# Gate product of the last mixer taken in three rounded passes, with the low weight parts subtracted on the Pool engine

## The chip, the cores and the metric

The kernel runs on one core of a Trainium2 chip. The metric is the device time of one execution in microseconds (us), as the median of several runs. The engines are named as in the profile: PE multiplies matrices, PEld loads its weights, DVE is the vector engine, ACT the scalar engine, POOL (GpSimd) the third elementwise engine, which here has issued DMAs only, and SP issues the weight transfers.

## The reference, cut to what matters

The model is two blocks on 256 tokens of width 1024. The change lies in the mixer of the second block. All its projections come from one input `h`:

```
h = rms_norm(x, attn_norm_g)
proj = h @ w_in
q, k, v, qi, ki, wi, glu_in, gates = jnp.split(proj, ...)
y_att = dsa_attention(q, k, v, qi, ki, wi, rel_bias) @ w_att_out     # top-64 keys per query, then softmax
y_conv = conformer_conv(glu_in, conv_w, conv_b, ...)                 # depthwise convolution with 31 taps
g = jax.nn.sigmoid(gates + b_gate).reshape(B, S, 2, D)
mixed = g[:, :, 0, :] * y_att + g[:, :, 1, :] * y_conv
x = x + mixed @ w_out
```

`gates` is a product of 256x1024 by 1024x2048. After the mixer comes a stage that gathers rows of expert tables (over a third of the time), then an embedding and the output.

## The kernel before, in words

Every engine runs a program of its own, written out by hand, and waits on semaphores. There is no scheduler: an instruction waits for all that stands ahead of it on its engine.

**Weights** are read through `ring`, four slots of 128x2048 f32, which SP fills in the order of `UNITS`. A unit is two slots, and the gates have four units. SP refills a slot when `raw_free` says that it was read.

**Two ways to multiply.** A product named in `SPLIT` is done in rounded type (fp32r): ACT copies a slot to `whi`, rounded (L499); DVE subtracts `wlo = ring - whi` (L1290), which also frees the ring slot; then PE adds three passes, high by high, low input by high weight, high input by low weight. The input's own parts, `hTh` and `hTl`, stand ready since the norm. `whi` and `wlo` have two buffers each, so slot q waits until the product of slot q-2 is over (`split_used`). In a product that is also in `WIDE`, one slot holds half of the inner dimension for 512 output columns, and each matmul has 512 columns (L809, function `wide`). The other way, which `gates` uses before the change, is a full f32 product straight from `ring` (L799), each matmul with 256 columns, after a one-row matmul that adds the bias (L1089).

**Around the gates.** PE's order is: last projection (`qkv`), gate block 0, transposes of q and k, gate block 1, first logits (L1110, L1113), gate block 2, transposes of the first probabilities, the second logits in two halves, gate block 3, transposes of the second probabilities, attention times v, then transposes of the convolution's result, and the two output projections (L1158). DVE meanwhile normalises q and k (L1663, L1664), picks the top 64 keys (L1677, L1678), runs 124 taps of the convolution (L1621, L1624) in stretches between the steps of the attention, adds the mask to the logits (L1705, L1713), finds the maximum, and normalises the probabilities (L1693). ACT takes the exponentials (L694) and the sigmoid of each gate block (L687). PE may start block n only after the sigmoid of block n-2. POOL has one load between (`conv_ln_b`), and the next (`ffn_norm_g`) is not needed before the gather stage.

## Time and profile before

| | us |
|---|---|
| median of 3 runs | 1884.62 |
| the runs | 1887.63, 1884.62, 1881.87 |
| profiled execution, its own time | 1888.51 |
| span of the profiled execution | 1886.5 |
| mean granted PE clock of its span | 0.938 |

Of the span PE is busy for 1569.8 us (83%), DVE for 1062.4 (56%), ACT for 526.2 (28%), POOL for 504.9 (27%). On the chain that ended last PE has 52%, POOL 15%, DVE 14% and DMA 10%. These are averages over stages with different limits; the change lies in the 100 us from 980 to 1080, and that stage is read by itself. A time in brackets at a timeline row's end is how long the engine sat idle before it, with what ended the idling. "x16" counts instructions in the trace: an f32 matmul stands in it as two instructions, a rounded one as one.

### The profile page before, as it was taken

Reading aid. Unit: us, or ns where it says so; the run is one execution under the profiler, and the core shown is the slowest. Engines: PE = TensorE matmul, PEld = TensorE weight load, DVE = VectorE, ACT = ScalarE, POOL = GpSimd, SP = SyncE. Lnnn points to the kernel's source line nnn. Section 1 sums busy time; section 2 is a strip of 40 time slices with the busy share of each in tenths; the row PEclk is TensorE's granted clock in tenths of the full one; section 3 lists DMA queues with packets and bytes.
Section 4 is the critical chain, followed back from the end, with each engine's and each line's share of the span. In section 5 each row is a group of like instructions: output and inputs, shape, how many; then the busy total and the mean of one; then the engine's idle time right before and its main releaser. Section 6 shows DMA issues by size and latency. Waiting matters only on the chain.

```text
span 1886.5 us, 19976 instructions
## 1 busy us (share of the span) xinstructions
PE 1569.8 (83%) x8015; PEld 1115.1 (59%) x8015; DVE 1062.4 (56%) x1762; ACT 526.2 (28%) x674; POOL 504.9 (27%) x555
## 2 busy tenths in 40 slices
PE   3998669999996869996999879838777776997787
PEld 2887569987985769985977548812222222442234
DVE  1642655644447446544388545596667566665553
ACT  2350145434442244434241212112121212212111
POOL 2000000000000000000000000557777776777771
PEclk8898789999998879997899999969999998999999
DMA  8548555556755445564343235999999999999994
GB/s 314 183 136 314 198 181 182 186 188 226 255 198 192 154 179 178 179 194 157 113 142 109 78 134 207 404 417 418 418 418 419 418 418 373 414 417 418 419 419 179
DMA packets 116259, 497.22 MB, mean 264 GB/s; under 512 B 12280, under 2 KB 12416, under 8 KB 98640
## 3 DMA queue, kind: packets, MB, share of 16 engines
q0 software_dynamic: 77424, 284.26, 37.5%
q1 hardware_dynamic: 38752, 211.83, 32.3%
q8 instruction: 55, 0.90, 0.2%
q14 instruction: 28, 0.23, 0.0%
HBM read 494.98 MB, written 1.06 MB: 263 GB/s over the span
## 4 chain that ended last, share of the span: by engine, by line
PE 52%; POOL 15%; DVE 14%; DMA 10%; issue 6%; ACT 2%; POOLq 0%; SPq 0%; DVEq 0%; ACTq 0%
PE G L799 21%; PE G L809 20%; POOL late L477 8%; DMA ybuf<-in_peer_u,mod 6%; POOL mod L477 3%; PE M L1202 2%; POOL arena L477 2%; DMA ring<-in_wpack 2%; POOL ybuf L477 2%; PE G L1158 2%; PE T L799 1%; DVE mod L1852 1%; DVE late L1852 1%; DVE wlo L1290 1%; PE G L837 1%
## 5 line engine op out<-in xcount | busy, mean ns | idle before, releaser
L1290 DVE TENSOR_TENSOR wlo<-ring,whi 128x2048 fp32r<-128x2048 f32 x120 | 274.9, 2292 | 313.5 <-ACT whi L499 313.2
L499 ACT ACTIVATE whi<-ring 128x2048 fp32r<-128x2048 f32 x120 | 229.3, 1911 | 365.2 <-PE G L809 185.4
L1202 PE MATMUL M<-late,cB 128*128 128x512 f32 x480 | 232.6, 613 | 46.7 <-DMA late<-in_peer_v,mod 46.7
L1852 DVE SCALAR_TENSOR_TENSOR late<-late,G 128x1024 f32<-128x1024 f32 x128 | 154.6, 1219 | 108.7 <-DMA late<-in_peer_u,mod 108.5
L1202 PEld LDWEIGHTS M<-late,cB 128*128 128x128 f32 x480 | 83.5, 189 | 193.4 <-DMA late<-in_peer_v,mod 125.1
L749 ACT ACTIVATE cB<-consts,mod 128x128 f32<-128x128 f32 x240 | 90.2, 398 | 357.7 <-PE M L1202 354.1
L1202 PE MATMUL M<-mod,cB 128*128 128x512 f32 x240 | 121.6, 635 | 74.3 <-ACT cB L749 48.5
L477 POOL DMA_INDIRECT late<-in_peer_u,mod x128 | 121.3, 948 | 51.1 <-issue 33.3
L477 POOL DMA_INDIRECT late<-in_peer_v,mod x128 | 122.0, 953 | 40.0 <-issue 36.1
L1202 PEld LDWEIGHTS M<-mod,cB 128*128 128x128 f32 x240 | 43.3, 197 | 149.9 <-issue 84.3
L799 PE MATMUL G<-hTh,whi 128*128 128x256 f32 x800 | 117.5, 291 | 10.8 <-DVE hTl L1311 7.3
L799 PE MATMUL G<-hTl,whi 128*128 128x256 f32 x800 | 115.8, 289 | 0.0
L799 PEld LDWEIGHTS G<-hTh,whi 128*128 128x128 f32 x800 | 107.5, 200 | 12.0 <-issue 11.9
L799 PE MATMUL G<-hTh,wlo 128*128 128x256 f32 x800 | 114.4, 287 | 0.0
L799 PEld LDWEIGHTS G<-hTl,whi 128*128 128x128 f32 x800 | 106.9, 198 | 0.0
L799 PEld LDWEIGHTS G<-hTh,wlo 128*128 128x128 f32 x800 | 105.4, 196 | 0.0
L1852 DVE SCALAR_TENSOR_TENSOR mod<-mod,G 128x1024 f32<-128x1024 f32 x64 | 76.4, 1218 | 33.5 <-DMA mod<-in_peer_u,mod 33.1
L809 PE MATMUL G<-whi,fl 128*128 128x512 f32 x320 | 88.4, 398 | 5.1 <-DVE fh L1589 5.1
L809 PE MATMUL G<-whi,fh 128*128 128x512 f32 x320 | 88.2, 398 | 0.0
L407 POOL DMA_DIRECT2D arena<-in_norm_g x4 | 2.1, 536 | 303.7 <-DVE arena L1515 156.1
L902 PE MATMUL T<-consts,ybuf 128*128 128x128 f32 x112 | 26.7, 417 | 61.3 <-ACT ybuf L537 41.8
L477 POOL DMA_INDIRECT mod<-in_peer_u,mod x64 | 60.1, 939 | 55.8 <-DVE mod L1835 27.1
(356 smaller groups left out, 2512.4 us busy)
## 6 DMA issues: line engine op xcount, KB each, us to landing
ring<-in_wpack SPq DMA_DIRECT2D x200, 1024.0 KB, 5.1
mod<-in_ada_b POOLq DMA_DIRECT2D x4, 512.0 KB, 9.3
arena<-in_norm_g POOLq DMA_DIRECT2D x4, 512.0 KB, 7.3
late<-in_peer_u,mod POOLq DMA_INDIRECT x128, 9.4
late<-in_peer_v,mod POOLq DMA_INDIRECT x128, 9.3
xs<-in_x SPq DMA_DIRECT2D x1, 1024.0 KB, 13.1
arena<-in_wsT POOLq DMA_DIRECT2D x1, 1024.0 KB, 5.0
mod<-in_ln_g POOLq DMA_DIRECT2D x1, 1024.0 KB, 9.5
```

Source lines behind the costliest of these rows:

```text
L407: pool.dma_start(dst, src).then_inc(sem(name), 16)
L477: nc.gpsimd.indirect_dma_start(out=rowbufs[j].rearrange("p a n -> p (a n)"), out_offset=None, in_=(A["peer_u"], A["peer_v"])[kind], in_off ...
L499: nc.scalar.activation(whi[:, q % 2, :], ring[:, raw % RING, :], ACT.Copy).then_inc(hi_done, 1)
L749: nc.scalar.activation(diags[:, k % DIAGS, :], ident, ACT.Copy, scale=actv[:, t, n:n + 1]).then_inc(sem("diag_made"), 1)
L799: ins = nc.tensor.matmul(dst, lhs(k), rhs(k), start=(first and k == 0), stop=(last and k == DC - 1))
L809: ins = nc.tensor.matmul(dst, lhs(t, k0 + k), w[:, :, k, :], start=(first and n + k == 0), stop=(last and n == 2 and k == 3))
L837: ins = nc.tensor.matmul(dst, cB[:, k, 0:32], w[:, :, k, :, r], start=(k == 0), stop=(k == DC - 1))
L902: return lambda dst: nc.tensor.transpose(dst[0:src.shape[1], :], src, ident)
L1158: ins = nc.tensor.matmul(G[:, b % 2, t, :], xT[:, k, t * P:(t + 1) * P], w[:, k, :], start=(k == 0), stop=(k == 3))
L1202: ins = nc.tensor.matmul(M[:, nb, :], diags[:, k % DIAGS, :], rowbufs[g % GBUF][:, nb, :], start=(n == 0), stop=(n == NSEL - 1))
L1290: V.tensor_tensor(wlo[:, q % 2, :], ring[:, raw % RING, :], whi[:, q % 2, :].bitcast(F32), ALU.subtract).then_inc(raw_free[raw % RING], 1)
L1852: V.scalar_tensor_tensor(out=row, in0=row, scalar=1.0, in1=G[:, t, :, :], op0=ALU.mult, op1=ALU.mult, accum_out=dots[:, t, n:n + 1]).then_ ...
```

## The change

`gates` joins `SPLIT` and `WIDE`, so that its eight slots are laid out and multiplied as the other rounded products are. PE adds the bias with one 512-column matmul for each of the two token tiles, then runs `wide` for each half. ACT rounds the slots, two ahead of each block. The subtraction is given to POOL, which does all eight one after the other, in its queue behind the load of `conv_ln_b`. DVE's counter of slots skips eight. In ACT's program the high parts and the sigmoids of the next blocks stand ahead of the exponentials.

```
-SPLIT = (..., "qi", "qkv", "glu",
-         "out")
-WIDE = ("a_v", "a_o", "a_out", "b_v", "qkv", "out")
+SPLIT = (..., "qi", "qkv", "glu",
+         "gates", "out")
+WIDE = ("a_v", "a_o", "a_out", "b_v", "qkv", "gates", "out")
@@ gpsimd
+            def low(name, j=0):
+
+                q, raw = SPLIT0[name] + j, 2 * UNIT0[name] + j
+                pool.wait_ge(hi_done, q + 1)
+                nc.gpsimd.tensor_tensor(wlo[:, q % 2, :], ring[:, raw % RING, :], whi[:, q % 2, :].bitcast(F32),
+                                        ALU.subtract).then_inc(raw_free[raw % RING], 1)
...
             load(clnb, A["conv_ln_b"].partition_broadcast(P), "l_cln")
+            for j in range(8):
+                low("gates", j)
             pool.wait_ge(m_free, SPARE0["att"])
@@ scalar
-            gate_sigmoid(0)
-            exponentials(0)
-            for nb in (1, 2):
+            split("gates", 0)
+            for nb in range(4):
+                if nb < 3:
+                    split("gates", nb + 1)
                 gate_sigmoid(nb)
-            exponentials(1)
-            gate_sigmoid(3)
+                if nb in (1, 2):
+                    exponentials(nb - 1)
@@ tensor, gate_product(nb)
+                for t in range(TT):
+                    nc.tensor.matmul(G[:, b % 2, t, :], ones[0:1, :], bgrow[0:1, 512 * nb:512 * nb + 512],
+                                     start=True, stop=False)
                 for half in range(2):
-                    h, c0 = 2 * (UNIT0["gates"] + nb) + half, 512 * nb + 256 * half
-                    w = raw(h)
-                    for t in range(TT):
-                        dst = G[:, b % 2, t, 256 * half:256 * (half + 1)]
-                        nc.tensor.matmul(dst, ones[0:1, :], bgrow[0:1, c0:c0 + 256], start=True, stop=False)
-                        ins = product(dst, lambda k: hT[:, k, t * P:(t + 1) * P], lambda k: w[:, k, :], False)
-                    ins.then_inc(raw_free[h % RING], 1)
+                    h = 2 * (UNIT0["gates"] + nb) + half
+                    pe.wait_ge(raw_free[h % RING], h // RING + 1)
+                    wide(b, SPLIT0["gates"] + 2 * nb + half, 4 * half, lambda t, k: hTh[:, k, t * P:(t + 1) * P],
+                         lambda t, k: hTl[:, k, t * P:(t + 1) * P], False, half == 1)
@@ vector, ahead of split("out", 0)
+            made[0] += 8
```

Gate block 0 on PE, between the last projection and the transposes of q (`T<-consts,arena`), in the kernel before:

```order
603 L1089 MATMUL G<-ybuf,ones 128x256
604 L799 MATMUL G<-ring,hT 128x256 x8
605 L1089 MATMUL G<-ybuf,ones 128x256
606 L799 MATMUL G<-ring,hT 128x256 x8
607 L1089 MATMUL G<-ybuf,ones 128x256
608 L799 MATMUL G<-ring,hT 128x256 x8
609 L1089 MATMUL G<-ybuf,ones 128x256
610 L799 MATMUL G<-ring,hT 128x256 x8
611 L902 MATMUL T<-consts,arena 128x128 x16
```

and in the changed kernel, where `wide` stands at L819 and the bias at L1095:

```order
603 L1095 MATMUL G<-ybuf,ones 128x512 x2
604 L819 MATMUL G<-whi,hTh 128x512 x4
605 L819 MATMUL G<-whi,hTl 128x512 x4
606 L819 MATMUL G<-wlo,hTh 128x512 x4
...
615 L819 MATMUL G<-wlo,hTh 128x512 x4
616 L912 MATMUL T<-consts,arena 128x128 x16
```

36 matrix instructions of 256 columns have become 50 of 512, 48 of them in rounded type. Each of the four blocks changes in this way.

ACT from the last copy of `qkv` (`arena<-G`) to the second set of exponentials, before; `mod<-G` is a sigmoid, `mod,small<-mod,small` an exponential:

```order
161 L681 ACTIVATE arena<-G 128x1024
162 L687 ACT_TABLE_LOAD
163 L687 ACTIVATE mod<-G 128x2x512
164 L694 ACT_TABLE_LOAD
165 L694 ACTIVATE mod,small<-mod,small 128x128 x8
166 L687 ACT_TABLE_LOAD
167 L687 ACTIVATE mod<-G 128x2x512 x2
168 L694 ACT_TABLE_LOAD
169 L694 ACTIVATE mod,small<-mod,small 128x256 x8
```

and after:

```order
161 L690 ACTIVATE arena<-G 128x1024
162 L508 ACTIVATE whi<-ring 128x2048 x4
163 L696 ACT_TABLE_LOAD
164 L696 ACTIVATE mod<-G 128x2x512
165 L508 ACTIVATE whi<-ring 128x2048 x2
166 L696 ACTIVATE mod<-G 128x2x512
167 L703 ACT_TABLE_LOAD
168 L703 ACTIVATE mod,small<-mod,small 128x128 x8
169 L508 ACTIVATE whi<-ring 128x2048 x2
170 L696 ACT_TABLE_LOAD
171 L696 ACTIVATE mod<-G 128x2x512
172 L703 ACT_TABLE_LOAD
173 L703 ACTIVATE mod,small<-mod,small 128x256 x8
```

The last two high parts stand behind the first exponentials.

POOL behind the load of the gate bias (`ybuf`), before:

```order
31 L407 DMA ybuf<-in_b_gate 1x16x128
32 L407 DMA arena<-in_conv_ln_b 128x512
33 L407 DMA mod<-in_ffn_norm_g 128x1024
34 L407 DMA arena<-in_skT 128x2048
```

and after:

```order
31 L407 DMA ybuf<-in_b_gate 1x16x128
32 L407 DMA arena<-in_conv_ln_b 128x512
33 L413 ISA
34 L413 TENSOR_TENSOR wlo<-ring,whi 128x2048 x8
35 L407 DMA mod<-in_ffn_norm_g 128x1024
36 L407 DMA arena<-in_skT 128x2048
```

Eight subtractions and one more instruction, which sets up the engine's code for them, stand between two loads.

## Rows read from the trace of the kernel before

**Rows 1.** Busy time by engine from 980 to 1080 us: busy, count, granted clock, DMA.

```profile
980.00:1080.00 100.00, 93.46 (x444) 68.92 (x444) 74.96 (x183) 20.25 (x44) 0.53 (x1) 1.00 0.26 90
```

**Rows 2.** PE's timeline: last slot of `qkv`, gate block 0, transposes, block 1.

```profile
974.55 1.07 PE L809 MATMUL G<-whi,hTh 128*128 128x512 f32 x4
...
980.09 0.69 PE L1089 MATMUL G<-ybuf,ones 1*128 1x256 f32 x2
...
997.09 1.04 PE L902 MATMUL T<-consts,arena 128*128 128x128 f32 x8
...
999.73 0.69 PE L1089 MATMUL G<-ybuf,ones 1*128 1x256 f32 x2
```

**Rows 3.** PE's timeline: the start and the end of gate block 2.

```profile
1023.50 0.69 PE L1089 MATMUL G<-ybuf,ones 1*128 1x256 f32 x2
...
1040.51 1.04 PE L902 MATMUL T<-consts,mod 128*128 128x128 f32 x8
```

**Rows 4.** PE's timeline: the two equal output projections, the first behind 3.44 us of idling.

```profile
1080.85 15.70 PE L1158 MATMUL G<-ring,arena 128*128 128x512 f32 x32
...
1101.03 14.00 PE L1158 MATMUL G<-ring,arena 128*128 128x512 f32 x32 [0.94 <-DVE arena L1283]
```

**Rows 5.** Busy time by engine over the first of these, as in rows 1.

```profile
1080.85:1096.50 15.65, 15.65 (x32) 6.59 (x32) 8.34 (x15) 4.56 (x5) 0.00 (x0) 0.89 0.21 67
```

**Rows 6.** DVE's timeline: start us, us, operation, and idling before it in brackets.

```profile
987.93 0.61 DVE L1677 MAX8 small<-arena 128x8 f32<-128x128 f32 x2
...
1000.51 15.12 DVE L1624 SCALAR_TENSOR_TENSOR mod<-arena,small,mod 128x256 f32<-128x256 f32 x38
...
1023.61 1.22 DVE L1705 TENSOR_TENSOR mod<-M,arena 128x1024 f32<-128x1024 f32 x1 [4.96 <-PE M L1113]
...
1041.14 1.29 DVE L1699 COPY arena<-T 128x512 f32<-128x512 f32 x2 [3.19 <-PE T L902]
1046.60 1.22 DVE L1713 TENSOR_TENSOR mod<-M,arena 128x1024 f32<-128x1024 f32 x1 [4.17 <-PE M L1113]
...
1073.25 6.41 DVE L1624 SCALAR_TENSOR_TENSOR mod<-arena,small,mod 128x256 f32<-128x256 f32 x16
```

**Rows 7.** ACT's timeline: a high part, and the last copy of `qkv`.

```profile
967.88 1.91 ACT L499 ACTIVATE whi<-ring 128x2048 fp32r<-128x2048 f32 x1 [3.52 <-PE G L809]
...
982.03 1.01 ACT L681 ACTIVATE arena<-G 128x1024 f32<-128x1024 f32 x1
```

**Rows 8.** Groups by form: busy us and mean ns of one, idle before.

```profile
L1290 DVE TENSOR_TENSOR wlo<-ring,whi 128x2048 fp32r<-128x2048 f32 x120 | 274.9, 2292 | 313.5 <-ACT whi L499 313.2
...
L1624 DVE SCALAR_TENSOR_TENSOR mod<-arena,small,mod 128x256 f32<-128x256 f32 x120 | 48.2, 477 | 0.0
...
L1419 DVE MEMSET small<- 128x1 f32 x1 | 0.1, 59 | 0.8 <-PEq L2011 0.8
...
L2011 POOL MEMSET const-uint8-127<- 128x1 uint8 x1 | 0.1, 115 | 0.0
...
L2011 POOL MEMSET const-float32-0.0<- 128x1 f32 x1 | 0.1, 98 | 0.2 <-issue 0.2
```

**Rows 9.** Single lines, ns: least/median/most: POOL's gathers, and DVE's casts.

```profile
L477 POOL DMA_INDIRECT late<-in_peer_u,mod x128: 933/937/1372, 1184.7 to 1804.8; - x128
...
L1803 DVE CAST mod<-mod x8: 189/192/325, 1169.4 to 1678.0; 128x64 f32<-128x64 uint32 x8
```

**Rows 10.** Timelines of POOL and DVE at two gathers that took long.

```profile
1211.35 1.37 POOL L477 DMA_INDIRECT late<-in_peer_u,mod  x1 [2.78 <-DVE late L1852]
...
1211.22 0.69 DVE L1804 TENSOR_TENSOR arena<-mod 128x512 f32<-128x512 f32 x1
...
1294.54 1.14 POOL L477 DMA_INDIRECT late<-in_peer_v,mod  x1 [0.30 <-issue]
...
1294.17 0.69 DVE L1816 TENSOR_TENSOR arena<-mod,consts 128x512 f32<-128x512 f32 x1
1294.90 0.69 DVE L1818 TENSOR_TENSOR mod<-arena,mod 128x512 f32<-128x512 f32 x1
```

## What the change was predicted to do

> **What bounds the kernel now.** I read busy time by stage first. From 980 to 1080 us PE is busy for 93.5 of 100 us, DVE for 75.0, ACT for 20, POOL for 0.5 [rows 1]. So PE looks like the limit and POOL like a free hand. Then I read the timelines, to see who waits for whom. PE starts the first three gate blocks at 980.09, 999.73 and 1023.50 and comes out of the third at 1040.51 [rows 2, 3], each 17 us long without a gap, while DVE waits for PE at each step of the attention: 4.96 us for the first logits, 3.19 for the transposed probabilities, 4.17 for the first half of the second logits [rows 6]. DVE's slack in this stage is thus about those waits and two later ones beside gate block 3, not the whole of the 25 us in which it is idle, and it is the only cushion for anything that holds DVE up. At the end of the stage comes a stretch of the convolution on DVE, the last of [rows 6], for which PE waits; all that follows (output projections, expert gathers) hangs on it and shifts with it.
>
> **PE's part.** A gate block takes 997.09 - 980.09 = 17.0 us now [rows 2]. Afterwards it has two halves of 24 rounded matmuls. The last slot of `qkv` is exactly such a half: 974.55 to 980.09 is 5.5 us [rows 2]. The bias is two f32 matmuls of 512 columns, four instructions in the trace; 32 such took 14.0 us [rows 4], so 1.75 us. A block is 1.75 + 2 x 5.5 = 12.75 us, 4.25 less than now, 17.0 us for the four. That is the gift, as far as PE stays the limit. The two operand parts of the input are there already and cost nothing.
>
> **ACT's part.** Eight high parts of 1.91 us [rows 7]. The first starts behind the copy of `qkv` at 982.03 + 1.01, so it ends at 985.0; it now stands ahead of gate block 0, which began at 980.09. The others run while ACT was idle (busy 20 of 100 us) and are hidden, but for their place: parts 6 and 7 stand behind the first exponentials, which follow the first mask on DVE. The refilled ring slots are no term: POOL frees a slot at least one product ahead of its reuse.
>
> **POOL's part: how long is one subtraction?** No row shows POOL doing elementwise work on a large tile. The low bound is DVE's own time for it, 2.29 us [rows 8]. For the high bound I scale by the one operation that both engines have in the trace, the one-element fill: 98 and 115 ns on POOL against 59 on DVE, 1.66 and 1.95 times as long [rows 8]. That gives 3.8 and 4.5 us; I take the middle, 4.1, nearest to these rows, and 2.3 to 4.5 as ends. The page "GPSIMD Engine Reference" of the Trainium skill (section 3.1) states 4497 ns for this operation and size; no run here shows it, and by it the sum below would be about 2.4 us higher. The setup instruction stands in the queue without a wait, 20 us ahead of the first subtraction: nothing, unless it takes longer than that.
>
> **Does POOL's work stop DVE?** Here is the term that decides. POOL's gathers take 937 ns, but some up to 1372 [rows 9]. The longest began at 1211.35, while DVE worked from 1211.22 to 1211.91 on an operation with two inputs in SBUF; it took 0.43 us too long. The one at 1294.54 took 0.20 too long, beside two such operations with 0.04 us between them [rows 10]. I looked up all gathers above 1.1 us: each lies beside a DVE operation with two SBUF inputs, and beside L1852, whose second input is in PSUM, they take 937. So POOL, reading its indices from SBUF, is held until such a DVE operation is over, and gets its turn at the boundary. The door seems to close the other way too: DVE's casts at L1803 take 192 ns, and one beside a gather 325 [rows 9]. A POOL subtraction, which reads two tiles throughout, should then hold DVE's two-input operations for its whole length. The rows bound this from below by 0 us (no two-input DVE row is visibly stretched, POOL's reads being short) and from above by the full length for each subtraction that meets such work. I take the full length, since the held gathers were held for all that was left of the DVE operation. The page "SBUF — State Buffer" of the Trainium skill (section "Who interferes with whom") says so for both directions: the first to start has the shared port for the whole instruction. The trace agrees for DVE holding POOL; for a two-input operation held by POOL no row here shows it.
>
> Which DVE work is of that kind? Normalising q and k (L1663, L1664) and the convolution (L1624), yes; the top-k (L1677, L1678), no, it has one input.
>
> **The sum**, with 4.1 us for each subtraction:
> 1. Subtractions 0 and 1 run from 985.0 on, into the normalising of k, and hold it: +8.2 us. Top-k ends 8.2 later, at 1006.0. Subtractions 2 and 3 start when PE has done products 0 and 1 (about 994.6 and 1000.1) plus a high part, at 996.6 and 1002.0, and lie under the top-k (10 us, one input): 0.
> 2. Gate block 0 ends about 1000.1 (989.1 + 11.0), before the top-k: no term. Block 1 ends near 1020.6, the first logits near 1027.3.
> 3. Subtractions 4 and 5 fall into the long stretch of the convolution (from 1000.51, 15 us and its tail [rows 6]): +8.2. The wait of 4.96 us before the first mask goes: DVE stands at +8.2 + 8.2 - 5.0 = +11.4.
> 4. Subtractions 6 and 7, by ACT's order, come behind the exponentials and fall into the 16 taps between normalising and the transposed probabilities: +8.2. The waits of 3.19 and 4.17 us go: +11.4 + 8.2 - 7.4 = +12.2 at the mask of the first half of the second logits.
> 5. From there PE leads again: the second half of the logits, then block 3, 4.25 us shorter: +12.2 - 4.25 = +8.0. The other three blocks' gain is spent in DVE's slack.
> 6. PE has then idled for some 10 us before those logits. What an idle stretch costs is seen in the two equal projections: 15.70 us behind a gap of 3.44, 14.00 behind a shorter one [rows 4], with a granted clock of 0.89 over the first [rows 5] against 1.00 over the whole stage before [rows 1]: part of it ran at the lower of the two levels. +1.7.
>
> Sum +9.7 us: 1898.2 against the profiled execution's own 1888.51. That execution is 3.9 above the median of the runs, 1884.62, so the median should be 1894.3.
>
> **Rivals.**
> (a) *Nothing holds DVE: faster.* Then only PE's chain counts. Block 0 starts its products at 985.0 + 4.1 = 989.1 and ends at 1000.1, 3.0 later than now; 7 us of idling before it cost 1.7; blocks 1 to 3 give 12.75. 3.0 + 1.7 - 12.75 = -8.1: 1876.5. DVE would still have 1 to 3 us of slack at each step, so the gain arrives. For it speaks that no two-input DVE row is stretched by a gather; against it, the gathers and the cast that were held. It decides at the door: if the subtractions and the taps run side by side at their own lengths, this is the case. With 4.1 us replaced by 2.3 or 4.5 it moves by -1.8 or +0.4.
> (b) *The door closes, but DVE keeps it.* The taps start every 0.398 us (15.12 / 38 [rows 6]) but last 0.477 [rows 8], so the next one is there before the last ends, and POOL may get in only where the run breaks. Then DVE loses little, and PE waits for POOL instead: subtraction 0 starts at 987.9, block 0 ends at 1003.1 (+6.0, with the clock +7.7), block 1 gives back 4.25, subtractions 4 and 5 wait for the end of the taps and cost some 2, block 2 gives 4.25, subtractions 6 and 7 cost 3 to 5 more at the step of the second logits, block 3 gives 4.25. About +1 with both ends, -2 to +5: 1886. Against it speaks the gather at 1294.54, which got in through a gap of 0.04 us.
> (c) *POOL is far slower than its rows suggest*, 6 us or more by code setup or rounding on write. Then each pair costs 12 and more, and the sum is +21 or above: over 1905.
>
> **How the numbers follow.** My forecast 0.50, (a) 0.17, (b) 0.27, (c) 0.06. The range goes from 1876 (half of (a)) to 1901 (the forecast with 4.5 us, +2.4, one more slow restart of PE, +1.7, and 2.5 for scatter of the runs, of which the three shown span 5.8). It leaves out (c) and half of (a). A measurement of this kernel can tell 0.3%, 5.7 us, from no change. (a) is beyond it on the fast side: faster 0.17. (b) and a small part of the forecast lie within: 0.30. The rest of the forecast and (c): slower 0.53.
>
> **What would show it.** In the changed kernel's trace: L819 halves of 5.5 us and bias of 1.75 (else the gift is wrong); POOL's subtractions and their length; DVE's L1624 stretches longer than 0.398 per tap by about 4 us at each of subtractions 4 to 7, and no wait left before the first mask (else the door is open, and (a) holds: the waits on DVE remain at 1 to 4 us and PE is busy without a gap); PE idle before the second logits. In (b), instead, POOL's subtractions would be long or late, ending where a run of taps ends, with PE waiting for `wlo`. The forecast is wrong if subtractions 4 to 7 meet DVE while it waits or does one-input work.

## The result: 1908.5 us, slower than before and beyond the range

The changed kernel takes 1908.5 us (median of 4 runs, 1907.9 to 1911.0) against 1886.1 us of the kernel before on the same chip: 1.0122 times as long, 95% interval 1.0098 to 1.0146. The forecast was 1894.3 with a range of 1876 to 1901. The direction was right and the size was not: +22.4 us in place of +9.7. The profiled execution took 1908.84 us, its span is 1907.0.

All times in this part are best read from one anchor, the start of the last unit (two slots) of `qkv` on PE. It stands at 968.99 us in the trace before and at 966.11 after. The stage ends where PE turns the convolution's tokens: 1079.71 before, 1096.98 after. So the stage grew from 110.72 to 130.87 us, by 20.15. PE's timeline of the changed kernel (start us, us, operation, idling before it in brackets):

```profile
966.11 1.17 PE L819 MATMUL G<-whi,hTh 128*128 128x512 f32 x4 [1.21 <-DVE wlo L1300]
...
986.58 2.07 PE L819 MATMUL G<-whi,hTh 128*128 128x512 f32 x4 [7.40 <-POOL wlo L413]
...
1006.88 1.94 PE L912 MATMUL T<-consts,arena 128*128 128x128 f32 x8 [6.87 <-DVE arena L1293]
1008.75 3.77 PE L1095 MATMUL G<-ybuf,ones 1*128 1x512 f32 x4
...
1061.34 1.22 PE L1120 MATMUL M<-arena 64*128 64x256 f32 x2 [8.51 <-DVE mod L1723]
...
1070.53 3.78 PE L1095 MATMUL G<-ybuf,ones 1*128 1x512 f32 x4
...
1087.16 1.04 PE L912 MATMUL T<-consts,mod 128*128 128x128 f32 x8
...
1096.98 1.09 PE L912 MATMUL T<-consts,mod 128*128 128x128 f32 x8 [3.44 <-DVE mod L1634]
1098.11 14.00 PE L1168 MATMUL G<-ring,arena 128*128 128x512 f32 x32
...
1116.60 17.00 PE L1168 MATMUL G<-ring,arena 128*128 128x512 f32 x32 [0.94 <-DVE arena L1293]
```

It waits 7.40 us inside gate block 0, 6.87 ahead of the turn of k and 8.51 ahead of the second half of the second logits. Before, the gate blocks had no gap [rows 2, 3], and the longest of the three waits was the last:

```profile
1047.88 0.70 PE L1110 MATMUL M<-arena 64*128 64x256 f32 x2 [1.31 <-DVE mod L1713]
```

The view by stretches of the changed kernel tells the same; its columns are those of [rows 1]:

```profile
980.00:1080.00 100.00, 78.04 (x261) 52.43 (x262) 89.39 (x158) 31.75 (x49) 40.09 (x9) 0.75 0.27 90
...
1061.30:1070.50 9.20, 9.16 (x16) 4.00 (x16) 0.00 (x0) 0.00 (x0) 0.00 (x0) 0.50 0.01 2
1075.00:1087.20 12.20, 12.20 (x49) 9.80 (x48) 6.61 (x13) 4.83 (x17) 0.00 (x0) 0.87 0.02 7
```

PE's share fell from 93.5 to 78.0, DVE's rose from 75.0 to 89.4, though DVE was given nothing to do, and the granted clock fell from 1.00 to 0.75. The second line is the second half of the logits: PE is busy throughout and has the lower level, 1.2 GHz, for all of it. The third is most of block 3, of which a part has the lower level too (0.87).

POOL's eight subtractions: the summary of line L413 (least, median, most ns) and their timeline.

```profile
L413 POOL TENSOR_TENSOR wlo<-ring,whi x8: 4497/4584/6683, 982.0 to 1049.0; 128x2048 fp32r<-128x2048 f32 x8
```

```profile
982.03 10.05 POOL L413 TENSOR_TENSOR wlo<-ring,whi 128x2048 fp32r<-128x2048 f32 x2 [22.11 <-ACT whi L508]
995.78 4.61 POOL L413 TENSOR_TENSOR wlo<-ring,whi 128x2048 fp32r<-128x2048 f32 x1 [3.70 <-ACT whi L508]
1001.21 4.50 POOL L413 TENSOR_TENSOR wlo<-ring,whi 128x2048 fp32r<-128x2048 f32 x1 [0.82 <-ACT whi L508]
1022.33 11.20 POOL L413 TENSOR_TENSOR wlo<-ring,whi 128x2048 fp32r<-128x2048 f32 x2 [16.61 <-ACT whi L508]
1043.76 4.66 POOL L413 TENSOR_TENSOR wlo<-ring,whi 128x2048 fp32r<-128x2048 f32 x1 [10.23 <-ACT whi L508]
1049.02 4.50 POOL L413 TENSOR_TENSOR wlo<-ring,whi 128x2048 fp32r<-128x2048 f32 x1 [0.60 <-ACT whi L508]
```

And DVE's timeline beside them, the answer to [rows 6]; and behind it, the summary of all single taps:

```profile
982.11 5.50 DVE L1673 TENSOR_TENSOR arena<-arena,small 128x1024 f32<-128x1024 f32 x1
987.64 5.51 DVE L1674 TENSOR_TENSOR arena<-arena,small 128x1024 f32<-128x1024 f32 x1
...
993.62 0.61 DVE L1687 MAX8 small<-arena 128x8 f32<-128x128 f32 x2
...
1003.00 3.00 DVE L1690 TENSOR_SCALAR arena<-arena 128x128 f32<-128x128 f32 x2
...
1009.46 15.13 DVE L1634 SCALAR_TENSOR_TENSOR mod<-arena,small,mod 128x256 f32<-128x256 f32 x38
1024.51 9.16 DVE L1631 TENSOR_SCALAR mod<-arena,small 128x256 f32<-128x256 f32 x2
...
1035.97 1.21 DVE L1715 TENSOR_TENSOR mod<-M,arena 128x1024 f32<-128x1024 f32 x1
...
1043.88 15.08 DVE L1634 SCALAR_TENSOR_TENSOR mod<-arena,small,mod 128x256 f32<-128x256 f32 x16
1058.88 1.27 DVE L1709 COPY arena<-T 128x512 f32<-128x512 f32 x2
1060.08 1.21 DVE L1723 TENSOR_TENSOR mod<-M,arena 128x1024 f32<-128x1024 f32 x1
...
1070.71 1.23 DVE L1723 TENSOR_TENSOR mod<-M,arena 128x1024 f32<-128x1024 f32 x1 [9.43 <-PE M L1123]
```

```profile
L1634 DVE SCALAR_TENSOR_TENSOR mod<-arena,small,mod x120: 469/477/4827, 959.7 to 1096.4; 128x256 f32<-128x256 f32 x120
```

Each normalising operation of k, 1.22 us when alone, takes 5.5 beside a POOL subtraction: it waits for the subtraction and then runs. The same holds for two single taps (the most is 4827 ns; the sixteen take 15.08 where they took 6.41 [rows 6]). The first mask (L1715), the copies (L1709) and the mask of the first half (L1723) no longer wait for PE. The waits of 4.96, 3.19 and 4.17 us in [rows 6] are gone. So the door is closed, as the prediction said, and subtractions 6 and 7 stretch the taps as it said they would. At 4 and 5 the picture is another. The run of 38 taps takes 15.13 us as before. What is held there are the two one-input scalings behind it, L1631, which take 9.16 us (in the kernel with all subtractions on DVE, below, they take 0.73). The scalings L1690 behind the top-k are held as well (3.00 us), and the prediction had put one-input work among what cannot be held. And POOL was kept out by the run of 38 taps, which is the rule of rival (b): a subtraction begun at 1022.33, 2.2 us before the run's end at 1024.51, took 6683 ns, 2.2 more than the least. Subtraction 7 was not kept out. It began at 1049.02, among the sixteen taps, and took 4.50 us.

### The profile page after: what moved, and what is told of

Read it like the earlier page. It is cut to its first block, busy times and chain, and to the rows that moved or that the text cites. A ratio compares the mean times of both kernels' runs of the same rounds, so it can differ in the third digit from the quotient of the medians.

```text
span 1907.0 us, 19839 instructions
## 1 busy us (share of the span) xinstructions
PE 1568.5 (82%) x7935; PEld 1108.4 (58%) x7935; DVE 1090.7 (57%) x1762; ACT 541.2 (28%) x682; POOL 546.3 (29%) x563
## 4 chain that ended last, share of the span: by engine, by line
PE 50%; DVE 17%; POOL 15%; DMA 10%; issue 6%; ACT 2%; POOLq 0%; SPq 0%; DVEq 0%; ACTq 0%
PE G L819 20%; PE G L809 19%; POOL late L486 7%; DMA ybuf<-in_peer_u,mod 5%; POOL mod L486 4%; PE M L1212 3%; DVE mod L1634 2%; POOL arena L486 2%; POOL ybuf L486 2%; DMA ring<-in_wpack 2%; PE T L809 2%; PE G L1168 2%; DMA mod<-in_peer_v,mod 1%; DVE mod L1863 1%; PE G L847 1%
## 5 line engine op out<-in xcount | busy, mean ns | idle before, releaser
L508 ACT ACTIVATE whi<-ring 128x2048 fp32r<-128x2048 f32 x128 | 244.5, 1911 | 395.6 <-PE G L819 223.7
L809 PE MATMUL G<-hTh,whi 128*128 128x256 f32 x800 | 116.8, 290 | 11.3 <-DVE hTl L1321 7.4
L819 PE MATMUL G<-whi,hTh 128*128 128x512 f32 x304 | 89.8, 420 | 14.7 <-POOL wlo L413 7.4
L819 PE MATMUL G<-whi,fl 128*128 128x512 f32 x320 | 88.7, 399 | 5.1 <-DVE fh L1599 5.1
L819 PE MATMUL G<-whi,fh 128*128 128x512 f32 x320 | 88.2, 397 | 0.0
L819 PE MATMUL G<-whi,hTl 128*128 128x512 f32 x304 | 85.8, 406 | 0.0
## 6 DMA issues: line engine op xcount, KB each, us to landing
xs<-in_x SPq DMA_DIRECT2D x1, 1024.0 KB, 13.1
```

The lines of the kernel that those rows point to most:

```text
L508: nc.scalar.activation(whi[:, q % 2, :], ring[:, raw % RING, :], ACT.Copy).then_inc(hi_done, 1)
L809: ins = nc.tensor.matmul(dst, lhs(k), rhs(k), start=(first and k == 0), stop=(last and k == DC - 1))
L819: ins = nc.tensor.matmul(dst, lhs(t, k0 + k), w[:, :, k, :], start=(first and n + k == 0), stop=(last and n == 2 and k == 3))
```

## Experiments

Sixteen kernels were run. The table gives for each its median, and its ratio to the kernel before on the same chip, with its interval. The other columns give how much later than before it reaches six points of the stage in its profiled execution, all counted from the anchor: DVE's top-k, the long run of taps, the first mask, the masks of the two halves of the second logits, and the end. Before, they stand at 18.94, 31.52, 54.62, 77.61, 84.09 and 110.72 us.

| kernel | median us | ratio (95%) | top-k | taps | mask 1 | half 1 | half 2 | end |
|---|---|---|---|---|---|---|---|---|
| changed | 1908.5 | 1.0122 (1.0098-1.0146) | +8.6 | +11.8 | +15.2 | +16.4 | +20.5 | +20.2 |
| e1_dve_low | 1893.9 | 1.0033 (1.0016-1.0049) | +4.4 | +10.1 | +9.5 | +3.2 | +6.4 | +7.1 |
| f1_pool03 | 1899.0 | 1.0054 (1.0034-1.0073) | +8.6 | +11.9 | +11.7 | +9.2 | +13.2 | +13.1 |
| f2_pool23 | 1893.1 | 1.0034 (1.0019-1.0050) | +4.4 | +6.0 | +7.5 | +4.3 | +6.8 | +6.6 |
| f3_pool47 | 1904.4 | 1.0084 (1.0056-1.0112) | +4.4 | +10.9 | +14.4 | +15.4 | +19.5 | +19.6 |
| e3_extra_sub | 1902.6 | 1.0076 (1.0052-1.0099) | +13.5 | +14.2 | +17.1 | +17.1 | +17.1 | +17.1 |
| e4_extra_fill | 1893.9 | 1.0046 (1.0026-1.0067) | 0.0 | +1.4 | +1.4 | +1.4 | +4.4 | +7.8 |
| e2_no_subtract | 1886.3 | 0.9992 (0.9975-1.0009) | 0.0 | +0.7 | -1.7 | -2.6 | +0.1 | -0.3 |
| e10_dense_bias | 1881.0 | 0.9982 (0.9962-1.0002) | 0.0 | 0.0 | -4.5 | -8.9 | -8.9 | -13.4 |
| e9_bias_middle | 1884.0 | 1.0005 (0.9989-1.0020) | 0.0 | +3.7 | +1.3 | -2.7 | +1.3 | -2.1 |
| e5_filler | 1900.7 | 1.0094 (1.0061-1.0127) | +8.6 | +11.3 | +14.6 | +15.7 | +15.7 | +13.2 |
| e6_half_ahead | 1900.8 | 1.0089 (1.0062-1.0117) | +8.5 | +12.7 | +16.1 | +17.1 | +18.3 | +13.7 |
| f4_filler_half | 1896.6 | 1.0048 (1.0033-1.0063) | +8.6 | +11.3 | +14.7 | +15.8 | +15.9 | +11.3 |
| e12_after_dense | 2002.7 | 1.0109 (1.0066-1.0151) | +8.5 | +12.6 | +16.1 | +17.1 | +21.2 | +17.7 |
| e7_mixed | 1981.6 | 1.0003 (0.9975-1.0030) | 0.0 | 0.0 | -2.5 | -2.5 | +0.3 | -0.2 |
| e11_mixed_dense | 1977.9 | 0.9988 (0.9955-1.0022) | 0.0 | +0.2 | -2.8 | -4.4 | -0.4 | -4.1 |
| e13_before_dense | 1980.9 | 1.0008 (0.9985-1.0031) | 0.0 | +0.3 | +0.1 | -1.5 | +2.2 | +1.8 |

e7, e11, e12 and e13 ran on a chip on which the kernel before takes 1979.9 us; the extra lies in the expert stage, and this stage has its usual length. Only their ratios are compared. The columns show one execution each. Those of f1 (1905.3 us) and e10 (1870.5) are the slowest and the fastest of their kernels, and that of e11 lies 7 us below its median, so these three columns show more than the medians do.

### Does a subtraction on POOL hold DVE? Two kernels without the split

e3: the kernel before, with eight unused subtractions on POOL. Nothing else is changed, but that DVE waits for them behind this stage.

```
+ pool.wait_ge(split_used, SPLIT0["out"])
+ for j in range(8):
...
+     nc.gpsimd.tensor_tensor(wlo[:, j % 2, :], xs..., xs..., ALU.subtract)
```

> The kernel before plus eight Pool subtractions of the same size (xs minus xs into the idle low buffer), for which nobody waits until long after the stage: four from the end of q's normalising, two from the 40th tap, two from the normalised first probabilities. PE's work is unchanged. Theory L: DVE's two-input operations stand still for 4.5 us at each subtraction that meets them (six of eight, two lying under the top-k), 27 us, less the waits of 5.0, 3.2 and 4.2 us, so +14.6 before the second logits, and PE idles and restarts slowly, +3 to +8: 1902 to 1910. Rival R: POOL's work in itself costs nothing, 1884 to 1888.

e4: the same with sixteen fills (`memset`) of the same tile, which write it and read nothing.

> The kernel before plus sixteen Pool fills of 128x2048 f32 at the same places as the extra subtractions: POOL writes and reads nothing. If only the reading side is shared with DVE's two-input work, the taps keep 0.398 us each and the time is that of before within 0.3%, 1881 to 1891. If POOL's work of any kind shuts DVE out, the taps stand still for the length of each fill and the time rises by most of the sum of the fills that meet them (12 of 16, 1.8 to 2.3 us each, less 12 us of waits: +10 or more).

The summary of the extra work, POOL's timeline of it, then DVE's timeline, in e3:

```profile
L467 POOL TENSOR_TENSOR wlo<-xs x8: 3595/3777/12092, 983.4 to 1050.9; 128x2048 fp32r<-128x2048 f32 x8
```

```profile
1019.61 15.70 POOL L467 TENSOR_TENSOR wlo<-xs 128x2048 fp32r<-128x2048 f32 x2 [19.95 <-DVE mod L1632]
1047.19 7.51 POOL L467 TENSOR_TENSOR wlo<-xs 128x2048 fp32r<-128x2048 f32 x2 [11.89 <-DVE mod L1701]
```

```profile
992.51 7.42 DVE L1682 SCALAR_TENSOR_TENSOR arena<-arena,consts 128x128 f32<-128x128 f32 x2
...
1013.12 15.12 DVE L1632 SCALAR_TENSOR_TENSOR mod<-arena,small,mod 128x256 f32<-128x256 f32 x38
1028.16 7.30 DVE L1629 TENSOR_SCALAR mod<-arena,small 128x256 f32<-128x256 f32 x2
...
1047.03 13.11 DVE L1632 SCALAR_TENSOR_TENSOR mod<-arena,small,mod 128x256 f32<-128x256 f32 x16
```

and the summary and DVE's timeline in e4:

```profile
L467 POOL MEMSET wlo<- x16: 1798/1804/1821, 980.8 to 1034.2; 128x2048 f32 x16
```

```profile
993.23 1.83 DVE L1687 TENSOR_SCALAR arena<-arena 128x128 f32<-128x128 f32 x2
...
1028.82 6.42 DVE L1631 SCALAR_TENSOR_TENSOR mod<-arena,small,mod 128x256 f32<-128x256 f32 x16
```

The subtraction alone, without any split, makes the kernel 0.76% slower, 1902.6 us, as expected from "the subtraction holds DVE": rival (a) is dead. Beside it sixteen taps take 13.11 us for 6.42, and beside fills they take 6.42. One subtraction started at 1019.61 inside the run of 38 taps and took 12.09 us, ending only after the run: rival (b)'s rule is real in that run, but when the run ends POOL gets in and DVE pays in full (7.30 for 0.73). Both engines lose. It is not a rule for every run of taps. At 1047.19 POOL began inside the run of sixteen, which had started at 1047.03, and got in at once: its two subtractions took 7.51 us together, little more than twice the least, and the taps stood still. What lets POOL in there and not in the run of 38 is not shown. e4 cost 0.46%, between the two cases I had written down. A fill held the scalings before the long taps (1.83 for 0.42 us) and DVE slipped by 1.4. In the traced execution the later columns grow to +7.8 without any DVE row being longer: PE ran at the lower level in the second half of the second logits and the start of block 3 (more on the clock below).

### Which of the eight? Four kernels with the split

e1 does all eight on DVE, at four places of its program; f1, f2 and f3 leave 0 to 3, 2 and 3, or 4 to 7 on POOL.

```
- for j in range(8):
-     low("gates", j)
...
+ split("gates", 0)      # DVE, after normalising k
...
+ split("gates", 1)      # after the copies of q and k
...
+ split("gates", 2)      # before the first mask
...
+ split("gates", 3)      # between the halves of the second logits
```

> The changed kernel with the eight subtractions on DVE, two behind the normalising of k, two behind the copies of q and k, two ahead of the first mask, two between the halves of the second logits. Theory L (a Pool subtraction of 4.5 us shuts out DVE's two-input work for its whole length, and the PE that waits restarts at half the clock): on DVE each costs 2.29 us and nothing is shut out, so the last convolution stretch comes 0 to 4 us earlier than before, 1883 to 1889 us; the longest stretches of L1624 keep their 0.398 us per tap. Rival R (the rounded product itself, the extra high parts on ACT and the later start of gate block 0 cost the time, whoever subtracts): within 5 us of the changed kernel, 1904 to 1912.

> The changed kernel's split with subtractions 0 to 3 on Pool and 4 to 7 on DVE; all else as with all eight on DVE (ratio 1.0033). Pool holds the two normalising operations 8.6 us where DVE's own two subtractions took 4.6: +4.0. Pair 2, 3 leaves DVE (-4.6) and holds its two one-input operations under the top-k (+2.6): -2.0. Theory of the trace (only the meeting counts): +2 against all on DVE, ratio 1.0040 to 1.0050, DVE's L1673 and L1674 at 5.5 us each, no stretched taps. If instead the first pair starts the whole loss (everything behind it late, PE at the low clock from its first wait on): ratio 1.007 and more.

> All subtractions on DVE but 2 and 3, which Pool does under the top-k. By the rows of the changed kernel the top-k's one-input operations run on undisturbed and only the two scalings behind it are held, 2.6 us; DVE is rid of 4.6. Expected 2 us less than with all on DVE: ratio 1.0015 to 1.0030. If Pool's subtraction holds the top-k in other ways, or DVE wasn't the limit there: 1.0033 or above.

> Subtractions 4 to 7 on Pool, 0 to 3 on DVE. Pairs 4, 5 and 6, 7 lie in the convolution: 8.4 and 8.7 us held in place of 4.6 each on DVE, +7.9 against all on DVE, and behind them the second half of the logits at the low clock, +4: ratio 1.0085 to 1.0100, the taps at 15.1 us per sixteen again and a tap of 4.8 us. If f1 and f3 each add to the all-on-DVE kernel what the trace says, the two together make the changed kernel's 16 us; if f3 comes out under 1.006, the pairs in the convolution are cushioned by PE's waits and the changed kernel's loss is at its beginning.

e1 missed its expectation (1893.9 us for 1883 to 1889), but it is 0.9% faster than the changed kernel: the same arithmetic, only the engine that does eight operations, and when it does them, differs. By the medians f1 adds 0.2% to it and f3 0.5%. The stage of f3, +19.6, is only 0.5 us below the changed kernel's: with the late pairs on POOL it matters little where the early ones are, since 8.6 + 2.6 us of holding stand against 2 x 4.5 of DVE's own work. The late pairs weigh most: f3 is slower than e1 with intervals that don't touch, f1 is not. By the medians f3 lies below the changed kernel (1.0084 and 1.0122), but the intervals overlap. f3's rows of POOL and DVE:

```profile
1013.08 16.73 POOL L413 TENSOR_TENSOR wlo<-ring,whi 128x2048 fp32r<-128x2048 f32 x2 [56.01 <-ACT whi L508]
```

```profile
1020.79 9.17 DVE L1631 TENSOR_SCALAR mod<-arena,small 128x256 f32<-128x256 f32 x2
```

POOL was 7.7 us earlier at the door than the run's end and got nothing from it, and DVE was held 8.4 us afterwards all the same. f2 missed: I had expected the pair under the top-k to be a gain of 2 us, and it gave none that the medians show. The timelines of POOL and of DVE in it:

```profile
1000.87 4.51 POOL L413 TENSOR_TENSOR wlo<-ring,whi 128x2048 fp32r<-128x2048 f32 x1 [0.83 <-ACT whi L508]
```

```profile
998.27 2.05 DVE L1691 TENSOR_SCALAR arena<-arena 128x128 f32<-128x128 f32 x2
...
1003.07 17.25 DVE L1634 SCALAR_TENSOR_TENSOR mod<-arena,small,mod 128x256 f32<-128x256 f32 x38
...
1047.44 1.23 DVE L1727 TENSOR_TENSOR mod<-M,arena 128x1024 f32<-128x1024 f32 x1 [4.17 <-PE M L1123]
```

The scalings lost 1.6 us and the first tap 2.1 (17.25 for 15.13), since the second subtraction ran until 1005.4. The top-k is 10 us long, but the high part for POOL's second subtraction comes only after its end. Still the traced run has DVE 2.0 us earlier at the first mask than e1 (+7.5 for +9.5), as I had expected. The lead is lost behind it, where DVE waits 4.17 us for PE: block 2 took PE 16.1 us from its bias to the next transposes, 14.5 in e1, more of it at the lower level.

### Where is the gift of PE? Three kernels without subtractions

e2 has the three passes with the high weights in the third; the low parts of the gate weights are left out of the product. e9 puts its bias between the two halves; e10 adds the bias as a product over 128 rows, of which all but the first are zero.

```
- nc.tensor.matmul(G[...], ones[0:1, :], bgrow[0:1, 512 * nb:512 * nb + 512], ...)
+ nc.tensor.matmul(G[...], ones[:, :], bgrow[:, 512 * nb:512 * nb + 512], ...)
```

> The changed kernel without the eight subtractions: POOL only passes the signal on, and the third pass multiplies by the high weight parts again, so PE's and ACT's work and order are unchanged and the low weight parts are missing from the gate product. Theory L: no lock, no wait for the low part; block 0 ends at 985 + 11 = 996, blocks 1 to 3 are 4.25 shorter each: 11 to 13 us faster than before, 1872 to 1876. Rival R: not faster than before, 1886 or more. This also gives what the three passes alone are worth.

> The kernel without subtractions (low weight parts missing), with the bias matmuls between the two halves of a gate block instead of ahead of it, so that dense matmuls follow the logits at once. Theory B: part of the lost clock comes back, 1877 to 1883. If the order of dense and one-row matmuls does not matter, and the logits alone bring the clock down: 1884 to 1888.

> The kernel without subtractions (low weight parts missing), with the bias matmuls taken over all 128 rows (rows 1 to 127 are zero) instead of one. Instructions, columns and order on PE are unchanged. Theory B (one-row bias matmuls behind the narrow logits leave the array almost unused, and this is what lets the granted clock fall in a stage in which PE never idles): the clock of the stage rises from 0.86 towards 1.0 and blocks 1 to 3 take 12.8 to 14 us instead of 14.6 to 16.6: 1876 to 1881. If rows in use do not matter: 1884 to 1888, as without this edit.

With no subtraction at all the gift of 17 us did not arrive: 0.9992. PE's timeline of e2 in the second logits, and its row by stretches from 1042 us:

```profile
1040.06 0.70 PE L1119 MATMUL M<-arena 64*128 64x256 f32 x2 [1.32 <-DVE mod L1722]
...
1042.00 1.22 PE L1122 MATMUL M<-mod,consts 128*128 128x256 f32 x2
...
1047.75 3.78 PE L1094 MATMUL G<-ybuf,ones 1*128 1x512 f32 x4
```

```profile
1042.00:1055.00 13.00, 13.00 (x23) 6.47 (x23) 7.00 (x12) 3.28 (x13) 0.54 (x1) 0.50 0.11 42
```

PE waited for no more than 1.32 us and yet went down to 1.2 GHz in the middle of the logits: a pair of narrow products took 1.22 us for 0.70, the bias 3.78 for 1.98. The block before them had run at 1.07 us per four. In e10's traced run the clock stayed at 1.00 over the whole stage (PE's timeline, and the stage in one stretch):

```profile
1034.52 0.70 PE L1124 MATMUL M<-mod,consts 128*128 128x256 f32 x2
1035.05 1.88 PE L1096 MATMUL G<-ybuf,ones 128*128 128x512 f32 x4
```

```profile
960.18:1057.51 97.33, 86.62 (x409) 64.25 (x409) 84.72 (x198) 38.57 (x56) 0.53 (x1) 1.00 0.33 114
```

and there the gift of blocks 1 to 3 is complete: 4.5 us each, 13.4 in all, 1870.5 us. But its ten runs lie between 1870.5 and 1886.6, two of them below 1877, with a median of 1881.0, and the ratio of 0.9982 is not told apart from that of e2. So the full bias by itself doesn't keep the clock up. e9 changed nothing by its ratio.

### The clock in the changed kernel

e5 throws products away on PE during its three waits. e6 moves the bias and the first half of block 3 ahead of the second half of the logits. f4 does e6 and the first two of e5's fillings. e12 has only the full bias.

```
+ filler(0, 28)                        # e5, f4: before block 0
...
+ if a == 1: filler(1, 28)             # e5, f4: before the turn of k
...
+ gate_product(3, (0,))                # e6, f4
  logits(2, 1, 4, 4)
- gate_product(3)
+ gate_product(3, (1,))                # e6, f4
```

> The changed kernel with dense matmuls whose results are thrown away in three places where PE waited: 28 ahead of gate block 0, 28 ahead of the transposes of k, 34 ahead of the second half of the second logits (each 512 columns, 0.23 us at full clock, so 6.4 to 7.7 us, inside waits of 7.4, 6.9 and 8.5 us). Theory C (of the 20 us lost, 8 are the low clock of the second logits' second half and of block 3, which come after PE has idled): those take 5.0 and 12.8 us instead of 9.2 and 16.6, and the time falls by 6 to 9 us against the changed kernel, to 1900 to 1903. If the clock has another cause: within 3 us of the changed kernel, 1906 to 1911.

> The changed kernel with the bias and the first half of gate block 3 moved ahead of the second half of the second logits, into PE's wait of 8.5 us. The work moved is 7.2 us at full clock. By theory C the clock stays up as well, so that the half left behind the logits takes 5.5 us and the end of the stage is bound by DVE's softmax (10.9 us behind the last mask): 9 to 12 us less than the changed kernel, 1897 to 1900. If moved work only takes the place of idling and the clock stays low: about 6 less, 1902.

> The changed kernel with both cures of PE's clock: products thrown away in its waits before block 0 and before the turn of the keys, and the bias and first half of block 3 moved ahead of the second logits' second half. Each alone gave 1.0094 and 1.0089 against 1.0122. With the lower clock gone everywhere (granted clock of the stage 0.95 or more) DVE's holds alone are left, 16 to 17 us less the 4 us that the earlier half block gives PE: 1.0065 to 1.0085. If it stays at 1.009, the second cure has nothing left to cure and DVE's holds are more than my 16.

> The changed kernel with its bias over 128 rows (rows 1 to 127 zero) and nothing else changed. In it PE runs at 1.2 GHz after each of its three waits of 6.9 to 8.5 us, and of the 22.4 us I put 6.3 to that clock beyond what I had forecast. If the bias, 3.8 us at the low clock, keeps the clock down: 1900 to 1904, as with products thrown away in the waits (1900.7). If the clock falls by PE's waiting and comes back by the products after it whatever the bias is: 1906 to 1910, no difference from the changed kernel.

PE's timeline in e5 from the second half of the second logits to the transposes behind block 3, and in f4 the same transposes:

```profile
1058.44 0.70 PE L1129 MATMUL M<-arena 64*128 64x256 f32 x2 [1.35 <-DVE mod L1733]
...
1063.46 1.98 PE L1101 MATMUL G<-ybuf,ones 1*128 1x512 f32 x4
...
1077.99 1.04 PE L912 MATMUL T<-consts,mod 128*128 128x128 f32 x8
```

```profile
1073.99 3.93 PE L912 MATMUL T<-consts,mod 128*128 128x128 f32 x16 [5.65 <-DVE mod L1714]
```

e5 computes nothing more of use and keeps all of DVE's holds. The logits ran at 0.70 us a pair, block 3 took 14.5 us for 16.6, and the end of the traced stage stands at +13.2 in place of +20.2. By the medians e5 is 0.3% faster than the changed kernel, and so is e6, which landed between its two expectations; the intervals of both still overlap that of the changed kernel. f4 is 0.74% faster, clear of it, and beat what I expected (1.0048 for 1.0065 to 1.0085). With half of block 3 done inside the wait, PE no longer sets the end of the stage: behind its last product of block 3 it waits 5.65 us for DVE's normalising. e12 shows no gain from the full bias (1.0109): in it the clock is low behind PE's waits whatever the form of the bias.

### The split only where nobody is held

e7 keeps blocks 0 and 2 in f32 and rounds 1 and 3, with block 1's subtractions on POOL right under the top-k and block 3's on DVE. e11 is e7 with the full bias, and e13 the kernel before with it.

```
+ pool.wait_ge(sem("dve_step"), MASKED)      # start of the top-k
+ for j in range(2):                         # low parts of block 1
...
+ if nb % 2:
+     ...                                    # three passes; even blocks as before
```

> The split done only where nobody is held. Gate blocks 0 and 2 stay f32 as before; blocks 1 and 3 are the rounded three passes. Block 1's two low parts are subtracted by Pool after the first mask, beside DVE's top-k (one input), block 3's by DVE between the two halves of the second logits. Three passes of a half took 5.5 us where f32 took 8.5, so the two blocks are worth 2 x 4.25 = 8.5 us of PE, of which DVE's two extra subtractions before the second half's mask may take 4.6 from the path in a stretch in which PE waited 4.2 to 5 us for it. If only the places of the subtractions made the changed kernel slow: 1876 to 1880 against 1885. If the lower clock takes back what PE saves, as with no subtraction at all (ratio 0.9992): 1884 to 1888, and the granted clock of the stage below 0.95.

> The kernel with the split in blocks 1 and 3 alone, and the bias of all four gate blocks added by a product over 128 rows, of which rows 1 to 127 of the bias tile are zero, so PE's array is full where it was fed one row. Instructions and their columns are the same. If the one-row bias and what follows it is where the clock falls: some 5 us less than the same kernel with the one-row bias, 1873 to 1879 against 1885. If the bias has no part in the clock: the same as that kernel within 2 us.

> The kernel before with only its gate bias over 128 rows (rows 1 to 127 zero). The control for the two others: before runs its stage at a clock of 1.00 in the profiled run, so a bias over all rows has nothing to win there: 1883 to 1887, ratio 0.998 to 1.002. A gain of 3 us or more would say that the spread of before's own runs (1879 to 1890) is this clock, too.

e7's two subtractions took 9.0 us under the top-k and held nothing: top-k and taps stand at 0.0. Block 1 gave 2.5 us at the first mask. Then the clock fell in the second logits as in e2, although block 2 ahead of them was f32, and the end is at -0.2. Its ratio of 1.0003 is what its trace says. e11 (0.9988) is no gain that its interval shows, and e13 shows that the full bias does nothing for the kernel before, in whose second logits the clock fell as well in this run (1.22 us a pair). No version beat the kernel before by more than the measurement tells.

## Why the prediction was wrong, and where it was right

The step that failed is step 6 together with step 5. The low clock of PE was put at one slow restart, 1.7 us, and block 3 at its full-clock length. Measured, the low level cost 8.1 us there: 4.2 in the second half of the logits and 3.9 in block 3. Against 1.7 that is 6.4 us too much, and from the first half's mask on the stage lost 6.3 more than forecast. The other 4.2 of the 10.5 us beyond the forecast lie ahead of it, with DVE: subtractions of 4.5 us for 4.1, and one-input scalings, put at 0, that were held.

- **What bounds the kernel** and **the door** (the term that the prediction called deciding): right. POOL's subtraction holds DVE's two-input operations for its whole length; e3 shows it by itself, e4 shows that a fill doesn't do that to the taps. Without the eight subtractions on POOL (e1) the loss shrinks from 1.22% to 0.33%.
- **PE's part**: right at full clock. A half took 5.45 us (993.52 to 998.97 in block 0), forecast 5.5, and the bias 1.98, forecast 1.75.
- **POOL's length**: 4.1 was taken, 4.50 measured when undisturbed (least 4497 ns). The row's upper end was right, and so was the Trainium skill (page "GPSIMD Engine Reference", section 3.1). Over three pairs: steps 1, 3 and 4 gave 8.57, 8.43 and 8.67 for 8.2 each, +1.1.
- **Step 1**: top-k 8.57 later, forecast 8.2. Right but for the length. "Subtractions 2 and 3 under the top-k: 0" was wrong: the list of what can be held counted only two-input operations. L1690 lost 2.6 us (3.00 for 0.42), and the copies of the keys came 0.7 later, since PE turned them at the low clock (1.94). At the long taps DVE stood at +11.8 for +8.2.
- **Step 3**: +8.43 for the held scalings, minus the wait of 4.96 (15.24 - 11.83 = 3.4; forecast 3.2). The size came out right by luck. The forecast had the taps held; they were not stretched, 15.13 as before, since POOL was kept out until the run broke, and the hold fell on the one-input scalings, which the forecast had counted as safe.
- **Step 4**: 8.67 - 3.19 - 4.17, +1.1 between the masks (forecast +0.8). So at the mask of the first half DVE is 16.4 late, forecast 12.2: the 4.2 us too many are the length (1.1) and the scalings and late copies behind the top-k (the rest).
- **Step 5**: block 3, from [bias 1070.53 to 1087.16] 16.6 us, forecast 12.75. The block was priced at full clock right behind PE's longest idling.
- **Step 6**: +1.7 for one slow restart. PE had three waits of about 7 us, and behind the last the low level lasted for the second half of the logits (9.2 us for 5.0, the windows row with 0.50), the bias (3.78 for 1.98) and the first products of the block. Steps 5 and 6 together gave +3.8 from the first half's mask to the end, where the forecast had 1.7 - 4.25 = -2.6: 6.3 us. e5 bears it out: with PE kept busy in its waits and the order unchanged, the step from half 1 to the end is 13.2 - 15.7 = -2.5, as the forecast had it.
- The sum: 9.7 + 4.2 + 6.3 = 20.2, the stage's 20.15. The medians differ by 22.4, 2.3 more. In the traced execution 3.2 us lie behind the stage: the two output projections took 14.00 and 17.00 for 15.70 and 14.00 [rows 4], +1.3, which is the clock again, the next rounded product took 1.2 longer, and the rest I did not split. (The span grew by 20.5 alone, since this execution reached the anchor 2.9 us earlier, in a part that the change doesn't touch.)
- **Rivals**: (a) fell with e3. (b)'s rule was right for the run of 38 taps and not for that of sixteen, and its conclusion was wrong, since POOL's turn comes at the run's end at DVE's cost. (c), 6 us or more, occurred in one subtraction (6683 ns), by waiting for DVE and not by slowness of its own.
- **Still open**: why the clock falls in e2 and e7 in the second logits behind waits of at most 1.32 us, and in the kernel before in its traced run does not. The full bias, the bias's place and the form of block 2 each don't decide it. Why POOL gets in among sixteen taps and not among 38 is open too. e1's own loss (the stage +7.1, granted clock 0.84 over it) was not split by an experiment. Its trace allows an estimate: from the second half of the logits (1042.91) to the end of block 3 (1068.81) PE took 25.9 us, and the same work at full clock is 5.0 + 12.8, 8.1 less. So the low clock of that stretch alone is as large as e1's loss.

## What to carry to other kernels

Before work is given to an idle POOL, list what DVE does beside it, also its one-input scalings, and charge each meeting with the full length of the POOL operation; a free POOL beside a DVE full of SBUF operations is no free hand, and DVE itself did the same subtraction in half the time. A gift on PE must be priced at the clock that PE will have after its waits are longer, not at the clock of before: the same 16.6 us block was promised as 12.75. Where a change makes PE wait, the wait also costs what PE does next: filling the waits with products thrown away (e5) shortened the traced stage by 7 us, and moving a piece of PE's queued work into the last wait (e6) by 6.

## What the runs showed of the hardware

- A POOL subtraction of 128x2048 f32 takes 4.50 us, 3.60 when both inputs are the same tile (e3), where DVE takes 2.29 for the first; a fill of that size takes 1.80 (e4).
- The exclusion of POOL and DVE goes both ways, as the Trainium skill has it ("SBUF — State Buffer", "Who interferes with whom"). A DVE operation was held up to 4.4 us, and a POOL one up to 8.5 us (12092 ns for 3595 in e3). Three subtractions begun inside the run of 38 taps, which follow each other without a pause, got in only at its end (here, in e3 and in f3); two begun among sixteen taps got in at once (at 1049.02 here, at 1047.19 in e3).
- One-input scalings of DVE are held as well, both by a subtraction (9.16 for 0.73) and by a fill (1.83 for 0.42); MAX8 and MATCH_REPLACE8 of the top-k are not, nor are copies out of PSUM (0.69 us each beside f2's second subtraction), nor two-input taps beside a fill.
- The setup instruction of POOL has 37 ns in the trace. It stands 22 us ahead of the first subtraction, so that anything it set off would have been hidden.
- PE's clock can fall to the lower level in the second logits behind a wait of only 1.32 us (e2, e7, e13), and it then costs several us: in e4 DVE was 1.4 us late and the traced stage ended 7.8 us late, the difference with the clock and not with work. That the 1.4 us brought the clock down is not shown.
